# Moving the first sixty steps of a written-out schedule: unit 2's queries, the projections and the attention of tile 1, four to eight gathers earlier

## The reference

```
x = x + concat(sparse_attention(rmsnorm(x)), retention(rmsnorm(x))) @ w_out
x = x + peer(rmsnorm(x))
y = rmsnorm(x)

def peer(h, ...):                                  # h: 128 tokens, 1024 wide
    q  = h @ w_query                               # 8 heads, 2 halves of 128
    v1, i1 = top_k(q[:, :, 0] @ keys1.T, 16)       # of 128 keys
    v2, i2 = top_k(q[:, :, 1] @ keys2.T, 16)
    top_s, sel = top_k(v1 + v2, 16)                # of 256 pairs
    e_idx = i1 * 128 + i2 of the 16 chosen pairs   # of 16384 experts
    act  = gelu(sum_d exp_u[e_idx] * h)
    return sum_k softmax(top_s) * act * exp_v[e_idx]
```

## Time and profile before

| | |
|---|---|
| median of 3 runs | 1176.54 us |
| profiled execution | 1174.26 us |
| its span | 1172.5 us |
| TensorE busy | 878.7 us (75%) |
| VectorE busy | 811.1 us (69%) |
| GpSimd busy | 545.0 us (46%) |
| ScalarE busy | 440.7 us (38%) |
| moved by DMA | 461.82 MB, mean 394 GB/s |
| of this gathered | 402.68 MB in 384 gathers |

### The profile page before, as it was taken

How to read it: one execution, slowest core, us unless ns; L and a number is a source line. 1 busy time by engine, 2 the same in 40 slices (tenths; PEclk the granted TensorE clock), 3 DMA queues, 4 the chain that set the end, 5 groups by cost and what they waited for, 6 DMA issues and landing times.

```text
span 1172.5 us, 12077 instructions
## 1 busy us (share of the span) xinstructions
PE 878.7 (75%) x3701; PEld 399.2 (34%) x3706; DVE 811.1 (69%) x2113; ACT 440.7 (38%) x1400; POOL 545.0 (46%) x431
## 2 busy tenths in 40 slices
PE   8999988998888757666668769477566667756654
PEld 6748643443333324222233333133122223211111
DVE  2425877877677889986777785648786777767543
ACT  2122444343443435423455563233333333333332
POOL 0002544563555555453654553545564555455441
PEclk9999999999898889776888999797988788776777
DMA  9902999999999999999999999999999999999995
GB/s 379 389 1 51 402 424 425 427 426 428 426 400 425 424 427 427 375 397 426 427 425 426 425 427 427 422 425 426 422 383 421 428 425 427 427 426 418 427 427 218
DMA packets 67057, 461.82 MB, mean 394 GB/s; under 512 B 8368, under 2 KB 10160, under 8 KB 15024
## 3 DMA queue, kind: packets, MB, share of 16 engines
q0 software_dynamic: 55296, 402.68, 82.2%
q1 hardware_dynamic: 11696, 58.37, 12.3%
HBM read 456.73 MB, written 3.24 MB: 392 GB/s over the span
## 4 chain that ended last, share of the span: by engine, by line
DMA 43%; PE 25%; DVE 16%; POOL 6%; issue 6%; ACT 3%; SPq 0%; DVEq 0%; POOLq 0%
DMA rows<-in_uv,ids 42%; PE ps L531 25%; DVE rows L1865 8%; POOL rows L498 4%; POOL work L483 2%; ACT work L1132 1%; DMA rows<-in_w_qi 1%; ACT wgt L1132 1%; ACT zact L1132 1%; DVE wt L1473 1%; DVE top L1469 1%; PE ps L534 1%; DVE work L1602 0%; DVE work L1598 0%; DVE work L1568 0%
## 5 line engine op out<-in xcount | busy, mean ns | idle before, releaser
L498 POOL DMA_INDIRECT rows<-in_uv,ids x384 | 453.1, 1180 | 490.6 <-PE ps L531 418.1
L531 PE MATMUL ps<-rows,work 128*64 128x512 f32 x1536 | 470.1, 743 | 278.6 <-ACT work L1132 278.2
L1865 DVE CUSTOM_DVE_ANT_0 rows<-rows,masks 128x1024 f32<-128x1024 f32 x256 | 313.7, 1226 | 157.3 <-DMA rows<-in_uv,ids 153.9
L1132 ACT ACTIVATE zact<-zdot 128x1 f32<-128x1 f32 x384 | 77.6, 202 | 583.2 <-DVE zdot L1865 583.0
L531 PEld LDWEIGHTS ps<-rows,work 128*64 128x64 f32 x1536 | 107.8, 157 | 544.4 <-ACT work L1132 382.1
L1865 DVE CUSTOM_DVE_ANT_0 rows<-rows,wt 128x1024 f32<-128x1024 f32 x128 | 157.0, 1227 | 89.6 <-DMA rows<-in_uv,ids 87.6
L531 PE MATMUL ps<-wt 128*128 128x128 f32 (+7 forms) x599 | 156.0, 414 | 0.9 <-DMA wt<-in_w_kv 0.9
L1132 ACT ACTIVATE work<-pair,wgt 128x64 f32<-128x64 f32 x384 | 133.5, 348 | 12.5
L1132 ACT ACTIVATE wgt<-zact,gates 128x1 f32<-128x1 f32 x384 | 113.1, 295 | 12.5
L531 PEld LDWEIGHTS ps<-work,wt 128*128 128x128 f32 (+1 forms) x712 | 95.0, 210 | 57.9 <-issue 57.9
L531 PE MATMUL ps<-work,wt 128*128 128x128 f32 (+1 forms) x712 | 108.7, 304 | 0.2 <-DMA wt<-in_w_q 0.2
(11 more groups left out here) (142 smaller groups left out, 632.8 us busy)
## 6 DMA issues: line engine op xcount, KB each, us to landing
wt<-in_w_q SPq DMA_DIRECT2D x9, 2048.0 KB, 13.3
rows<-in_uv,ids POOLq DMA_INDIRECT x384, 12.6
rows<-in_w_out SPq DMA_DIRECT2D x2, 2048.0 KB, 32.2
wt<-in_w_out SPq DMA_DIRECT2D x2, 2048.0 KB, 11.4
wt<-in_ckv SPq DMA_DIRECT2D x16, 256.0 KB, 11.3
x<-in_x SPq DMA_DIRECT2D x5, 512.0 KB, 8.6
rows<-in_w_qi SPq DMA_DIRECT2D x1, 2048.0 KB, 13.0
wt<-in_w_qa SPq DMA_DIRECT2D x1, 2048.0 KB, 10.9
```

The source lines that it names most:

```text
L498: pool.indirect_dma_start(row[s], None, a["uv"], bass.IndirectOffsetOnAxis(ap=ids[:, own(n // KP).start + n % KP:own(n // KP).start + n % ...
L531: return nc.tensor.matmul(out, lhsT, rhs, start=start, stop=stop)
L1132: return nc.scalar.activation(*args, **kw)
L1865: V.tensor_tensor_reduce(row[s][:, 0:D], row[s][:, 0:D], h2r[t % 2][:, n % 2, :], 1.0, 0.0, ALU.mult, ALU.add, zdot[:, s:s + 1]).then_inc( ...
```

## The change

Nothing is computed that was not computed before; the numbers that place the pieces change, and with them the order on TensorE, ScalarE, VectorE and GpSimd. Unit 2's queries move from step 8 to steps 4 and 6, unit 3's are spread over four steps and lose their place among the hurried ones, the projections start 2 to 4 steps earlier, tile 1's exponentials are split into two pieces, `later_qa(1)` and ScalarE's `later_qa(0)` come before the first add, and the ids of unit 1 are made and spread earlier. The core of the diff:

```diff
-        AHEAD, HURRIED, FAST = (1, 2, 15, 16), (2, 3, 8, 16), (2, 3, 16, 17, 18)
+        AHEAD, HURRIED, FAST = (1, 2, 15, 16), (2, 8, 16), (2, 3, 16, 17, 18)
         def q_at(u):
-            return {2: 8, 3: 10, 4: 20, 8: 88, 16: 224, 17: 230}.get(u, 16 * u - 48)
+            return {2: 4, 3: 10, 4: 20, 8: 88, 16: 224, 17: 230}.get(u, 16 * u - 48)
         def take_at(u):
-            return q_at(u) + (3 if u == 2 else 5 if u in HURRIED else 11)
+            return q_at(u) + (5 if u in HURRIED else 11)
         def scores_at(u):
-            return {2: 10, 3: 24, 4: 34, 16: 232, 17: 248}.get(u, 16 * u - 34)
+            return {2: 12, 3: 24, 4: 34, 16: 232, 17: 248}.get(u, 16 * u - 34)
         def spread_at(u):
-            return {1: 6, 2: 22, 15: 228, 16: 244}.get(u, 16 * u - 10)
+            return {1: 2, 2: 24, 15: 228, 16: 244}.get(u, 16 * u - 10)
...
@@ TensorE, before the loop
             later_qa(0)
             query_scores(1)
+            later_qa(1)
             pe.wait_ge(qi_sb, 3)
             y_start(0)
             add_experts(0)
-            later_qa(1)
-            add_experts(2)
             pe.wait_ge(scored, 2)
             later_qa(2)
             later_qa(3)
-            add_experts(4)
+            add_experts(2)
...
@@ TensorE, in the loop
-                        if part == 7 or part == 3 and u > 3 or part % 2 and u not in HURRIED:
+                        if part % 4 == 3 or part % 2 and u not in HURRIED:
                             yield
...
-            PROJECTIONS = ((14, "qkb", 1, 3), (24, "vb", 1, 3), (30, "vb", 2, 2),
-                           (36, "gb", 1, 3), (42, "qkb", 2, 2), (48, "gb", 2, 3))
+            PROJECTIONS = ((10, "qkb", 1, 3), (20, "vb", 1, 3), (26, "vb", 2, 2),
+                           (32, "gb", 1, 3), (38, "qkb", 2, 2), (46, "gb", 2, 3))
...
@@ retention_1 on TensorE: until 26, 32, 38, 48 become 22, 28, 34, 46
@@ attention_1 on TensorE: until 6, 14, 18 become 4, 12, 16; index_2: 54 becomes 50
-                if n > 4:
+                if n > 2:
                     add_experts(n, n % (HP * KP) == HP * KP - 2)
...
@@ ScalarE
             take_q(1)
+            later_qa(0)
...
-                yield from until(11)
+                yield from until(9)
                 exps_1(0)
+                yield from until(12)
                 exps_1(1)
...
             for n in range(4):
                 weigh(n)
-            later_qa(0)
-            for n in range(4, 6):
-                weigh(n)
             later_qa(1)
...
@@ ScalarE's copies of the projections: 33, 39, 45, 57 become 29, 35, 41, 55
@@ VectorE
                 yield from until(3)
-                for i, _ in enumerate(top16(1)):
-                    if i % 4 == 3:
-                        yield
+                whole(top16(1))
...
-                yield from until(10)
+                yield from until(11)
+                scale_probs(1, prob1[:, 0, :, :], 0, 4)
                 row_max(2, [ps[:, b, :].rearrange("p (j n) -> p j n", j=2) for b in (0, 3)], 4, 4)
                 yield from until(15)
-                scale_probs(1, prob1[:, 0, :, :], 0, 4)
-                yield
                 scale_probs(2, prob1[:, 1, :, :], 4, 4)
...
@@ retention_1 on VectorE: until 23, 36, 42, 47, 50, 58 become 20, 32, 38, 44, 47, 54
@@ GpSimd: the small operations after gathers 48 and 50 come after 44 and 46
```

More of the change, by code:

```diff
@@ L504, in _ @@
                     gate_exp(gates_after[n])
-                if n == 48:
+                if n == 44:
                     group_rstd(1)
-                if n == 50:
+                if n == 46:
                     pool.wait_ge(o_ps, 2)
@@ L856, in projections @@
                     w, s = {"qkb": (w_qkb, qk_ps), "vb": (w_vb, vb_ps), "gb": (w_gb, gb_ps)}[name]
-                    if start == 14:
+                    if start == 10:
                         pe.wait_ge(expd, 3)
-                    if start == 24:
+                    if start == 20:
                         pe.wait_ge(rotated, 2)
-                    if start == 30:
+                    if start == 26:
                         pe.wait_ge(pv_sb, 3)
-                    if start == 36:
+                    if start == 32:
                         pe.wait_ge(vb_sb, 2)
-                    if start == 42:
+                    if start == 38:
                         pe.wait_ge(vb_sb, 3)
-                    if start == 48:
+                    if start == 46:
                         pe.wait_ge(gb_sb, 2)
@@ L892, in retention_1 @@
             def retention_1():
-                yield from until(26)
+                yield from until(22)
                 pe.wait_ge(rotated, 2)
@@ L897, in retention_1 @@
                 last.then_inc(rt_ps, 1)
-                yield from until(32)
+                yield from until(28)
                 pe.wait_ge(rt_sb, 2)
@@ L905, in retention_1 @@
                 last.then_inc(s_ps, 1)
-                yield from until(38)
+                yield from until(34)
                 pe.wait_ge(s_masked, 2)
@@ L920, in retention_1 @@
                 last.then_inc(sp_ps, 1)
-                yield from until(48)
+                yield from until(46)
                 mix_t(1)
@@ L1043, in attention_1 @@
                 scores_1(0)
-                yield from until(6)
+                yield from until(4)
                 scores_1(1)
-                yield from until(14)
+                yield from until(12)
                 prob_t1(0)
-                yield from until(18)
+                yield from until(16)
                 values_1(0)
@@ L1062, in index_2 @@
             def index_2():
-                yield from until(54)
+                yield from until(50)
                 pe.wait_ge(rotated, 3)
@@ L1267, in natural @@
             def natural():
-                for start, dst, t, bank, s, done, func in ((33, vb, 1, 3, vb_ps, vb_sb, ACT.Copy), (39, vb, 2, 2, vb_ps, vb_sb, ACT.Copy),
-                                                           (45, gs, 1, 3, gb_ps, gb_sb, ACT.Silu), (57, gs, 2, 3, gb_ps, gb_sb, ACT.Silu)):
+                for start, dst, t, bank, s, done, func in ((29, vb, 1, 3, vb_ps, vb_sb, ACT.Copy), (35, vb, 2, 2, vb_ps, vb_sb, ACT.Copy),
+                                                           (41, gs, 1, 3, gb_ps, gb_sb, ACT.Silu), (55, gs, 2, 3, gb_ps, gb_sb, ACT.Silu)):
                     yield from until(start)
@@ L1320, in background @@
             def background():
-                yield from until(11)
+                yield from until(9)
                 exps_1(0)
+                yield from until(12)
                 exps_1(1)
-                yield from until(19)
+                yield from until(16)
                 prob_t1(0)
-                yield from until(22)
+                yield from until(20)
                 values_1(0)
@@ L1330, in background @@
                 values_1(1)
-                yield from until(29)
+                yield from until(26)
                 act.wait_ge(rt_ps, 2)
                 copy(rT1, bank4(0)).then_inc(rt_sb, 1)
-                yield from until(44)
+                yield from until(41)
                 act.wait_ge(sp_ps, 1)
@@ L1339, in background @@
                     ins.then_inc(sp_sb, 1)
-                yield from until(53)
+                yield from until(51)
                 mix_take(1)
@@ L1718, in next_spreads @@
                 for u in range(1, UNITS):
-                    yield from until(spread_at(u) + (3 if u > 1 else 4))
+                    yield from until(spread_at(u) + (3 if u > 1 else 2))
                     spread_take(u)
@@ L1744, in retention_1 @@
                 decayed(kdn1, 1)
-                yield from until(42)
+                yield from until(38)
                 dve.wait_ge(o_ps, 2)
                 o_stats(1, 0)
+                yield from until(44)
+                o_normed(1, 0)
                 yield from until(47)
-                o_normed(1, 0)
-                yield from until(50)
                 dve.wait_ge(vb_sb, 3)
                 yield from rotate(2, 2, cs_b[:, 1], prod)
-                yield from until(58)
+                yield from until(54)
                 dve.wait_ge(w_ps, 3)
```

6 lines of the change are left out of this document (3 added, 3 removed).

## The result

The changed kernel takes 1187.99 us (median of 4 runs, 1186.80 to 1192.39) against 1176.74 us of the kernel before (4 runs): ratio 1.0106, interval 1.0076 to 1.0137. It is slower, by 11.3 us of medians. The profiled execution is a fifth run, and faster than all four: 1183.61 us, span 1181.8, against 1174.26 and 1172.5. So the traces account for 9.3 us; the other 2 us lie in runs that no trace shows.

A forecast was written before the change was run, and what follows sets the result against it. The DMA engines were taken to bound the kernel. Add 38 11.6 us later meant 9.2 us of stream gaps, net 8.8: profiled 1183.1, median 1185.3, forecast 1184 us; own range 1180 to 1189, overall 1176.5 to 1190.

The forecast's parts named there:

- The bound and the price: DMA stream bounds the time; each microsecond TensorE is late at add 38 beyond 2.4 us is lost.
- The margin: At add 38, which frees gather 46's place: TensorE may be 2.4 us later before the stream runs dry.
- Ahead of the loop: Add 0 starts at 131.4 instead of 126.1, TensorE idles 1.9 us before it; cost on the stream: nothing.
- Unit 1's ids: GpSimd's wait of 3.71 us ahead of gather 16 goes; stream already full behind it, so worth nothing.
- Unit 2's queries: Behind add 4: wait of 0.9 us for weight load 1; add 8 ends at 159.4, some 8 us later.
- Exponentials: TensorE waits 4.5 us at add 10, 2.3 at the first projection; add 14 ends at 181.0, before 170.3.
- The first gap: Stream gaps of 1.8 us at gather 20 and 2.4 at gather 22; first part of the loss 4.2 us.
- Weight load 2: Issued at 186.8, lands about 197.3; TensorE idles 4.4 us at step 20, bounds 0 and 7.
- Earlier projections: Ahead of add 38: 8.2 us of extra TensorE work from projection parts and retention's outputs and states.
- The sum: From 124 us to add 38: idle 16.8 against 13.4, plus 8.2 of work; add 38 ends 11.6 us later.
- a rival of 0.09: Work behind TensorE's waits runs at half clock: add 38 another 8 to 10 us late, time 1193; chance 0.09.
- the ring: Rival: waits overlap, add 38 up to 5.8 us late, loss 0 to 3.5, time about 1178.5; chance 0.22.

The follow-up runs named there:

- work6: Kernel before plus 6 extra matmuls that nobody reads, at the piece of step 30 (5.3 us of work); 1176.44 us, ratio 1.0023.
- work12: Kernel before plus 12 extra matmuls that nobody reads, at the piece of step 30 (10.4 us of work); 1182.83 us, ratio 1.0073.
- preloop: Kernel before with only the part of the change that lies ahead of the loop; 1176.12 us, ratio 1.0010.
- fill_after: Changed kernel with matmuls of zeros where TensorE waits ahead of adds 4, 10 and 20, zero tile 4 bytes per partition; 1201.67 us.
- proj_back: Changed kernel with the projections from the first `vb` on and retention back at their old places; 1182.12 us, ratio 1.0062.
- query_back: Changed kernel with unit 2's queries back at step 8, their copy at 11 and tile 1's exponentials joined there; 1192.72 us, ratio 1.0153.
- hurry3: Changed kernel with unit 3's queries hurried again, so that weight load 2 is issued earlier; 1188.87 us, ratio 1.0108.
- the four fill kernels: Kernel before and changed kernel, each with matmuls of zeros where TensorE waits, zero tile of 4 or 64 bytes per partition; 1187.35 to 1201.67 us.
- fill_before: Kernel before with matmuls of zeros ahead of adds 52, 58 and 74, zero tile 4 bytes per partition; 1190.97 us.
- fill_before_64: Kernel before with matmuls of zeros ahead of adds 52, 58 and 74, zero tile 64 bytes per partition; 1187.35 us.
- proj_early: Kernel before with the projections from the first `vb` on, retention and copies at their new places; 1184.96 us, ratio 1.0089.

## Why the prediction was right, and where it was not

**The bound and the price** were right. The forecast was 1184 and the time 1188.0, inside its range of 1180 to 1189 but near its end. The sum made on the profiled execution gave 1183.1, and that one took 1183.6; as it was the fastest of five runs, that it hit so closely is luck in part. One microsecond of lateness at add 38 costs about one of stream: over nine kernels with lateness from 0.8 to 21.5 us, the missing time that was added is the lateness less 2.0 at most and 0.5 more than it at least. The times by the medians follow within some 3 us.

**The margin** of 2.4 us was near in time and too large on the stream: by work6 and work12 it is about 2 us of time, and 0.5 to 0.7 us of missing time up to 300 us. That a further microsecond or so comes back behind the stretch was not in the sum. The margin was worked out from bytes and a delay of 2 us from add to data that no row gives better than to a microsecond.

**Ahead of the loop**: add 0 at 131.29 for 131.4, the idle 2.05 for 1.9, load 1 issued at 140.36 for 140.5. Nothing was predicted for it, and preloop has 1.6 us, with an interval from 0 to 2.2.

**Unit 1's ids**: GpSimd's wait for the gates ahead of gather 16 is gone, and worth nothing, as the steps had it. Gathers 12, 14 and 16 now wait for TensorE alone:

```profile
150.60 0.94 POOL L498 DMA_INDIRECT rows<-in_uv,ids  x1 [5.87 <-PE ps L531]
...
155.94 0.94 POOL L498 DMA_INDIRECT rows<-in_uv,ids  x1 [2.91 <-PE ps L531]
...
160.29 0.94 POOL L498 DMA_INDIRECT rows<-in_uv,ids  x1 [2.17 <-PE ps L531]
```

**Unit 2's queries**: the wait of 0.9 for load 1 did not come, because add 4 before it took 3.31 us and not 1.94. Add 8 ended at 159.5 for 159.4.

**Exponentials**: the wait before add 10 was 4.87 for 4.5. Add 10 ended at 168.06 for 165.8: it took 3.68 us. The wait of 2.3 for `expd` did not come, the exponentials were done at 169.7 and TensorE came at 169.86 behind slow query parts. Add 12 ended at 174.75 for 173.7, add 14 at 181.6 for 181.0.

**The first gap** was 4.2 us at 170 to 190; it is 3.9 in 168 to 192. Not foreseen were 1.9 us at 152 to 160, a window at 323 GB/s:

```profile
152.00:160.00 8.00, 7.51 (x45) 3.74 (x43) 2.61 (x6) 3.14 (x8) 2.91 (x3) 1.00 0.95 323
```

Twelve gathers and load 1 are 14.7 MB, and by the windows 14.6 had passed at 152 us, when gathers 12 and 13 had just been issued; 14 and 15 followed at 155.9, behind the slow add 4 and half the queries. The prediction asked the stream at gathers 20 and 22 and not at 12 and 14.

**Weight load 2** was issued at 187.40 for 186.8. The wait was 0 where 4.4 stood, because the wait for ScalarE of 3.48 and the slow add 20 came first. fill_after shows 1.68, proj_back 3.94, so the term of 4.4 was too large but not imaginary. TensorE used it at 198.02 without a wait, so it was at most 10.7 us under way. The row's 10.6 fits here. The estimate of 11.8 by the rule of the Trainium skill (DMA: Bandwidth & Descriptors, "Queues, rings and completion order"), that a DMA engine takes turns between its queues, is too long for this trace, though the gathers beside the load ran nearly full (418 GB/s from 187.4 to 198 us). In other traces the same load took 10.8 us (fill_after), 11.5 (query_back), 12.0 (hurry3) and 12.1 (proj_back) from issue to landing. So the estimate lies inside what was measured, and neither value can be called the right one.

**Earlier projections**: 8.2 us of work ahead of add 38. TensorE's busy time grew by 11.75: these 8.2, and 3.6 more at the low clock than before. The three slow adds and the query parts and the projection behind add 10 add up to 5.6 us over their full-clock times; the kernel before had about 1.7 us of the same kind, behind its wait of 2.3 us before add 10.

**The sum, and the step that failed**: idle time of 16.8 us was forecast against 13.4; it is 13.9. The 3.4 us more were 0.5, and in their place stand 3.6 us of matmuls at the low clock, which the sum had left to a rival of 0.09. 8.2 + 3.4 = 11.6 was forecast, 8.2 + 0.5 + 3.6 = 12.3 came. That the two errors cancel is not all luck: a slow add uses up the wait that would have come behind it, as fill_after shows the other way round. But the sum was right for a wrong reason in this term, and as a rule for the parts it fails: proj_back, by its terms 3.4 us late, was 10.2 late in its trace.

**What was given back**: 0.4 us at 140 to 152 was near (0.8 has become 0.6). The prediction said that nothing later changes. Yet a gap at 336 to 356 us closed, first before, then after:

```profile
300.00:380.00 80.00, 71.56 (x259) 27.57 (x260) 60.74 (x156) 32.89 (x108) 42.39 (x33) 0.88 1.00 416
336.00:356.00 20.00, 16.21 (x69) 5.81 (x65) 16.38 (x41) 10.79 (x35) 15.54 (x11) 0.91 0.98 383
```

```profile
300.00:380.00 80.00, 70.45 (x267) 26.71 (x269) 63.04 (x164) 36.88 (x115) 45.48 (x34) 0.94 1.01 422
336.00:356.00 20.00, 17.36 (x70) 6.70 (x70) 16.50 (x41) 8.93 (x29) 11.67 (x9) 1.00 1.02 426
```

From 300 to 380 us together that is 80 x 6/427 = 1.1 us, and 10.5 us more missing up to 300 less 1.1 is 9.4, the 9.3 of the span. What closed the gap is open. work12, which moves nothing, has 420 for 416 from 300 to 380 us, which would speak for the lateness itself; but proj_back, as late, has 412, and 385 in the gap.

**The rivals**: the ring did not hide it. The clock did fall, 0.98 to 0.94 and not under 0.9, and cost 3.6 us, not 8 to 10. The faster rival lived on later gaps; from 300 to 380 us they gave back 1.1 us, a tenth of what was lost.

## What to carry to other kernels

Where a stream of transfers bounds the time, find the spot with the least margin and price a change of order by one number, how late the release at that spot comes; early work, waits and low clock enter through it (of the three, work was tried alone). Do not add up waits in a list one by one: behind each stretched one, the next shrinks, so two parts of a change that each cost 8 to 10 us cost 11 together here. Measure a disputed margin with idle work in the kernel before: work6 and work12 changed one thing only, and are the cleanest evidence here.

## What the runs showed of the hardware

**The gather's rate and the place of the buffer.** In the four fill kernels the full rate of the stream was 418 to 422 GB/s for the whole program, against 425 to 428 in the others. The window from 160 to 228 us, first before, then fill_before, then fill_before_64:

```profile
160.00:228.00 68.00, 58.71 (x274) 28.16 (x274) 55.98 (x152) 29.06 (x100) 36.66 (x26) 0.98 1.01 427
```

```profile
160.00:228.00 68.00, 59.30 (x271) 27.21 (x270) 54.85 (x151) 28.64 (x98) 36.45 (x26) 0.97 1.01 420
...
281.64 2.11 PE L533 MATMUL ps<-ident_bf,zeros_bf 128*128 128x512 bf16 x9
```

```profile
160.00:228.00 68.00, 57.78 (x270) 27.29 (x271) 55.47 (x151) 28.19 (x96) 36.65 (x26) 0.99 1.01 421
```

The first matmul of zeros ran at 281.64, long after: the matmuls are not the cause. What differs from the start is one small tile in front of the gather buffer (with the instruction that sets it to zero, and one more wait of TensorE at the start). It moved the buffer from byte 32,512 of each partition to 32,544 and 32,576, and all tiles behind it by as much, the row numbers and the weights among them. By the rate alone, 7/427 of some 1,030 us of gathers is 17 us; fill_before lost 16. The theory that a multiple of 64 bytes is enough fell: 32,576 is one. 32,512 is also a multiple of 256 and the other two are not. The Trainium skill (DMA: Bandwidth & Descriptors, "How a descriptor splits into AXI transactions") says that the pieces into which a transfer is split start at 256-byte boundaries, so that one which starts off a boundary can need one more: its example of 576 bytes takes three pieces from a boundary and four off it. The page tells it of the bytes that are fetched, and here it is the written side that moved. It fits the direction, but a kernel with the buffer at another multiple of 256 was not run, and the other tiles that moved were not held apart. So this cause stays open.

**The clock of short stalls.** Behind waits of 2.8 to 4.9 us the add that followed took 3.3 to 3.7 us instead of 1.94 in the changed kernel; behind one of 2.05 (add 0) it took 1.94, in proj_back 3.53 at the same place. In preloop add 0 took 2.54 behind the same 2.05. Nor does a longer wait decide it: add 16 of the kernel before took 1.94 us behind a wait of 3.01, and add 16 of proj_early 1.94 behind 3.23. So waits of 2 to 3.2 us can go either way, even at one place of one order, and a term for the low clock needs both ends; behind the waits of 3.5 to 4.9 us ahead of add 38 it came each time, in whole or in part.
